# A four-layer mixer with float32 products: layer norm roots computed with tokens on partitions and spread by TensorE, scaled chunks in a ring, the final norm's sums gathered during layer 1's output projection

## The chip, the core and the metric

The program runs on one core of one Trainium2 chip. The metric is the device time of one execution in microseconds (us); lower is better.

## What is computed

256 latent tokens and 256 context tokens (512 in all) of width 2048 go through four layers. Two layers come from a first block, then its output is normed once more (`final_g`), and two layers of a second block follow, with a fresh context. Each layer begins with the same modulated norm of both halves:

```
h_lat = rms_norm(x,  norm_g[l]) * (1.0 + scale)   + shift
h_ctx = rms_norm(xc, norm_g[l]) * (1.0 + scale_c) + shift_c
...                                  # input projections, attention, gates
x  = x  + gate   * (mixed @ w_out[l])
xc = xc + gate_c * (mixed_c @ w_out[l])      # not in a block's last layer
...
return rms_norm(x, final_g)          # end of the first block
```

`rms_norm(x, w)` is `x * rsqrt(mean(x * x) + 1e-6) * w`, with the mean over the 2048 features of a token. So between two layers there are three steps: a sum of squares over all features, one inverse root for each token, and a product with every element.

## The kernel before

Activations are held with features on partitions: `x_residual` (xT) is 16 chunks of 128 features by 512 tokens, context tokens first. Each product with a weight is done in three passes for precision (a high and a low part of both operands), `three`, L1294. Weights come in slots of 128x1024 elements: the sync engine (SP) loads a slot into `w_raw` (a ring of 4), ScalarE (ACT) copies it to `w_high` (L547, `high(n)`), VectorE (DVE) subtracts to get `w_low` (L849, `low(n)`), and TensorE (PE) multiplies. `w_high` and `w_low` are rings of 2, so that `high(n)` waits until PE has used slot n-2. A group of four slots makes two output tiles. Every engine has its own stream, written out in the order of the list of phases that `plan_phases` makes; semaphores tie the streams together.

Between layers the phases are these:

- `linear` "out" (four rounds of two groups). After each group DVE adds the gated result to xT (L1170), squares two chunks (L1181) and adds them to a running sum in `tmp` (L1185). After the last group it folds two halves into one (L1221), and PE multiplies the sum by a matrix of ones (L1563): this sums over partitions and leaves the sum in every partition of PSUM `scores`, 128x512.
- `store` writes xT's latent half to `x_scratch` in device memory (ACT's queue, L824), to be read back in the next layer's `ysplit`.
- `root`: ACT makes mean and root of all 128x512 elements (`mean_and_root`, L559 and L560), DVE takes the reciprocal and one Newton step (`inverse_root`, L876 to L887).
- `apply`, for each of 16 chunks: DVE scales xT in place (`scale_chunk`, L922), ACT adds the shift and makes `h_high` (L605), DVE makes `h_low` (L932). Weight slots 1 to 5 of the next projection are split in between (`split_beside`).

The order of layer 1's end is longer. A root for the final norm, the final norm's product with all 16 chunks (L1108), the store, then a new pass of squares over the normed x (phase "ms": ACT L738, PE L1499, 16 chunks in turn), then the root of layer 2.

In `opening` the first layer does the same with squares from ACT (L623) and 16 products with ones (L1514), in between the first modulation products (L1345, L1355); the copy L555 stands on ACT behind the first shifted chunks and two weight slots.

The first q projection's round takes its slots in the order `PAIRED`; its slots 0 to 5 are split ahead, and the slot with index 6 is split by the first `high` and `low` behind `apply`:

```
for k in range(8):
    if 8 * i + k >= ph["ahead"]:
        high(n0 + 8 * i + k + 1)
```

## Time and profile before

| | us |
|---|---|
| runs shown, median (lowest to highest) | 3244.1 (3240.6 to 3244.69) |
| the profiled execution, its own time | 3241.01 |
| its span in the trace | 3239.1 |
| PE busy | 3027.7 (93% of the span) |
| DVE busy | 1605.7 (50%) |
| ACT busy | 1023.4 (32%) |
| POOL busy | 102.0 (3%) |

The span is the stretch from the first to the last instruction of the profiled execution. PE is busy nearly throughout. All rows below are from that one execution; their times are us from the span's start.

### The profile page before, as it was taken

How to read it: one execution, taken by the hardware profiler on the slowest of the kernel's cores; microseconds unless marked ns; L12 is line 12 of the kernel's file. 1: busy time of each engine (PE TensorE's matmuls, PEld its weight loads, DVE VectorE, ACT ScalarE, POOL GpSimd, SP SyncE). 2: the span in 40 equal slices, each digit the busy share in tenths (PEclk: the TensorE clock that was granted, in tenths of full speed). 3: DMA queues.
4: the chain of work that ended last, by engine and by line, in shares of the span. 5: the costliest groups of instructions: out<-in, count | busy, mean ns of one | idle time of the engine just before them, and what ended most of it. 6: DMA issues, size and time to landing. Idle time of an engine off the chain costs nothing. (4 is left out here: it accounts for less than half of the span.)

```text
span 3239.1 us, 40895 instructions
## 1 busy us (share of the span) xinstructions
PE 3027.7 (93%) x17158; PEld 2362.8 (73%) x17158; DVE 1605.7 (50%) x2493; ACT 1023.4 (32%) x1508; POOL 102.0 (3%) x157
## 2 busy tenths in 40 slices
PE   5899999999997999999878999999999979999988
PEld 1577777785675787886766779766776758798888
DVE  2334333355435554454556373555473455747574
ACT  2212233223312332332323221334342123315453
POOL 0000000000000000000000000240000000003100
PEclk7899999999998999999989999999999989999999
DMA  8644433221543643741763444333445433222455
GB/s 321 274 169 143 144 130 130 98 73 45 183 174 137 227 176 121 268 132 65 272 225 126 154 151 166 132 111 111 150 158 206 163 116 117 85 92 92 137 169 169
DMA packets 120135, 495.10 MB, mean 153 GB/s; under 512 B 11792, under 2 KB 30480, under 8 KB 95120
## 3 DMA queue, kind: packets, MB, share of 16 engines
q1 hardware_dynamic: 99648, 463.51, 40.2%
q10 hardware_dynamic: 20304, 28.97, 2.6%
q8 instruction: 136, 2.23, 0.3%
q14 instruction: 47, 0.39, 0.0%
HBM read 484.05 MB, written 8.39 MB: 152 GB/s over the span
## 5 line engine op out<-in xcount | busy, mean ns | idle before, releaser
L1294 PE MATMUL products<-h_high,w_high 128*128 128x512 f32 (+1 forms) x3424 | 1256.2, 367 | 91.4 <-DVE h_low L932 47.1
L1294 PE MATMUL products<-h_low,w_high 128*128 128x512 f32 (+1 forms) x3424 | 1189.7, 347 | 0.0
L1294 PE MATMUL products<-h_high,w_low 128*128 128x512 f32 (+1 forms) x3424 | 1189.2, 347 | 0.0
L849 DVE TENSOR_TENSOR w_low<-w_raw,w_high 128x1024 fp32r<-128x1024 f32 x500 | 615.3, 1231 | 819.6 <-ACT w_high L547 817.1
L547 ACT CAST w_high<-w_raw 128x1024 fp32r<-128x1024 f32 x500 | 522.9, 1046 | 1382.4 <-PE products L1294 1333.8
L1294 PEld LDWEIGHTS products<-h_high,w_high 128*128 128x128 f32 x3424 | 657.3, 192 | 341.9 <-issue 228.0
L1294 PEld LDWEIGHTS products<-h_low,w_high 128*128 128x128 f32 x3424 | 659.0, 192 | 81.0 <-issue 13.0
L1294 PEld LDWEIGHTS products<-h_high,w_low 128*128 128x128 f32 x3424 | 657.4, 192 | 81.6
L1294 PE MATMUL products<-w_high,h_high 128*128 128x256 f32 x640 | 184.1, 288 | 0.5 <-issue 0.5
L1294 PE MATMUL products<-w_high,h_low 128*128 128x256 f32 x640 | 181.1, 283 | 0.0
L1294 PE MATMUL products<-w_low,h_high 128*128 128x256 f32 x640 | 181.0, 283 | 0.0
L876 DVE RECIPROCAL tmp<-tmp 128x512 f32<-128x512 f32 (+2 forms) x35 | 133.3, 3809 | 76.4 <-ACT tmp L560 76.4
L1369 PE MATMUL modulation<-ada_w,cond_silu 128*32 128x512 f32 x1264 | 169.0, 607 | 0.0
L670 ACT ACTIVATE tmp<-scores,softmax_stats,q_root 128x512 f32<-128x512 f32 (+1 forms) x144 | 101.5, 708 | 174.5 <-DVE softmax_stats L1017 174.5
L1294 PEld LDWEIGHTS products<-w_high,h_high 128*128 128x128 f32 x640 | 122.7, 192 | 13.1 <-issue 12.3
L1294 PEld LDWEIGHTS products<-w_high,h_low 128*128 128x128 f32 x640 | 122.8, 192 | 1.0 <-issue 1.0
L1294 PEld LDWEIGHTS products<-w_low,h_high 128*128 128x128 f32 x640 | 122.7, 192 | 0.0
L1010 DVE TENSOR_REDUCE softmax_stats<-scores 128x1 f32<-128x512 f32 (+1 forms) x144 | 86.0, 597 | 60.9 <-PE scores L1436 37.5
L1023 DVE RECIPROCAL softmax_stats<-softmax_stats 128x1 f32<-128x1 f32 x192 | 26.5, 159 | 163.7 <-ACT tmp L670 163.7
L510 POOL COPY pool_values<-mix_a 128x512 f32<-128x512 f32 (+1 forms) x16 | 12.2, 765 | 2912.1 <-DVE mix_a L1159 2910.7
L657 ACT COPY tmp<-turned 128x512 f32<-128x512 f32 (+1 forms) x96 | 49.3, 514 | 169.2 <-PE turned L1448 169.2
L605 ACT ACTIVATE h_high<-x_residual,ada 128x256 fp32r<-128x256 f32 x128 | 56.7, 500 | 90.3 <-DVE x_residual L922 90.3
(193 smaller groups left out, 2676.9 us busy)
## 6 DMA issues: line engine op xcount, KB each, us to landing
w_raw<-w_slots SPq DMA_DIRECT2D x500, 512.0 KB, 3.5
ada_w<-ada_slots SPq DMA_DIRECT2D x174, 1024.0 KB, 6.0
mix_b<-ada_slots SPq DMA_DIRECT2D x18, 1024.0 KB, 9.8
x_residual<-x ACTq DMA_DIRECT2D x2, 4096.0 KB, 23.0
x_scratch<-x_residual ACTq DMA_DIRECT2D x3, 2048.0 KB, 8.0
x_residual<-x_scratch ACTq DMA_DIRECT2D x3, 2048.0 KB, 9.2
x_residual<-ctx ACTq DMA_DIRECT2D x2, 2048.0 KB, 16.2
out<-x_residual ACTq DMA_DIRECT2D x1, 2048.0 KB, 7.8
```

What stands on the lines that cost most here:

```text
L510: step(nc.gpsimd.tensor_copy(pool_v[:, seg, PAD:PAD + S], v))
L547: nc.scalar.copy(whi[:, n % SPL, :], raw[:, n % RAW, :]).then_inc(high_done, 1)
L605: last = nc.scalar.activation(hh[:, t, tk], xT[:, t, tk], ACT.Identity, bias=adaT[:, r, c + st:c + st + 1])
L657: nc.scalar.copy(dst[:, 0:nk], src[:, 0:nk]).then_inc(pt_done, 1)
L670: nc.scalar.activation(tmp[:, t0 + c % ring, 0:nk], src, ACT.Exp, scale=a["scale"] if a["wide"] else q_rs[:, k:k + 1], bias=stat[:, c % 8, ...
L849: nc.vector.tensor_tensor(wlo[:, n % SPL, :], raw[:, n % RAW, :], whi[:, n % SPL, :].bitcast(F32), ALU.subtract).then_inc(low_done, 1)
L876: step(nc.vector.reciprocal(r, r))
L1010: step(nc.vector.reduce_max(stat[:, c % 8, 0:1], src, AX.X))
L1023: step(nc.vector.reciprocal(stat[:, c % 8, 3:4], stat[:, c % 8, 2:3]))
L1294: ins = nc.tensor.matmul(o, a, b, start=first and q == 0, stop=last and q == 2, skip_group_check=skip)
L1369: ins = nc.tensor.matmul(AD[32 * j:32 * j + 32, :], sc32[:, k, :], place[:, j * 512:(j + 1) * 512], start=k == 0, stop=k == KC - 1)
```

## The change

1. **Sums.** A matmul has one operand held in the array (the weights) and one that moves through it. Before, the ones were held and the squares moved, 512 columns. Now each 128x128 tile of squares is held and one column of ones moves (`token_sums`): a token's sum lands on one partition, and the sums of 512 tokens are 128x4 numbers.
2. **Roots.** Mean, root and inverse are computed on 128x4 numbers. PE then spreads them to all partitions, with a column of `x_root` repeated as the held operand and the identity moving (`x_broadcast`), and ACT copies the 128x512 result from PSUM to `tmp`.
3. **Last group of an output projection.** Its two chunks are not added to the running sum. ACT squares one, DVE the other, and PE sums them directly; the fold L1221 is gone. ACT issues a small root ahead, on `eps`.
4. **Ring.** `scale_chunk` writes to a ring of four pieces of `tmp` (`xs`) and leaves xT as it was. The wait for the store moves from `apply` to the kv or k projection.
5. **Final norm.** During layer 1's output projection ACT also squares each latent chunk times its final gain, and DVE adds these to `gained` (in `pool_sums`). From the two sums DVE gets the combined inverse root of both norms for the latent half, and the final norm's own. The phases "ms" and one of the two roots are gone. The final norm's product with xT (16 instructions) and the store now stand behind layer 2's `apply`.

The core of the diff (semaphores, tiles and phase bookkeeping are left out):

```diff
+            def x_root(layer):
+
+                n = 6 if layer == 2 else 4
+
+                nc.scalar.activation(stat[:, 7, 3:4], eps_col[:, 0:1], ACT.Sqrt)
+                act.wait_ge(x_var, layer + 1)
+                nc.scalar.activation(x_rs[:, 0:n], x_ms[:, 0:n], ACT.Sqrt).then_inc(x_rooted, 1)
+
+                act.wait_ge(x_spread, layer + 1)
+                nc.scalar.copy(tmp[:, 2, :], SC[:, 1, :]).then_inc(x_ready, 1)
...
@@ -748,6 +737,10 @@
                     for t in range(KC):
                         shift_chunk(layer, t, at["apply"] + t + 1)
                         split_beside(pi, t, high)
+                    if layer == 2:
+
+                        act.wait_ge(x_final, KC)
+                        act.dma_start(dram["x_scratch"], xT[:, :, LAT]).then_inc(x_out, 16)
                 elif kind == "linear":
...
+                        if ph["evac"] == "res" and ph["layer"] == 1:
+
+                            g = 2 * i + j
+                            if g > 1:
+                                act.wait_ge(x_gain_sum, g - 1)
+                            for t in range(2):
+                                c = COL["final"] + 2 * g + t
+                                if g < 2 * ph["pairs"] - 1:
+                                    act.wait_ge(freed_dve, 2 + at["fd"] + g + 1)
+                                else:
+                                    act.wait_ge(x_tile, 2 * ph["layer"] + t + 1)
+                                    if t == 0:
+
+                                        nc.scalar.activation(tmp[:, 0, :], xT[:, 2 * g, :],
+                                                             ACT.Square).then_inc(x_tile_sq, 1)
+                                dst = gained[:, t, :] if g == 0 else tmp[:, 4, t * S:(t + 1) * S]
+                                nc.scalar.activation(dst, xT[:, 2 * g + t, LAT], ACT.Square,
+                                                     scale=cols[:, c:c + 1]).then_inc(x_gained, 1)
+                            return
+                        if ph["evac"] == "res" and ph["layer"] < LAYERS - 1 and 2 * i + j == 2 * ph["pairs"] - 1:
+
+                            act.wait_ge(x_tile, 2 * ph["layer"] + 1)
+                            nc.scalar.activation(tmp[:, 0, :], xT[:, 4 * i + 2, :], ACT.Square).then_inc(x_tile_sq, 1)
+                            return
...
             def scale_chunk(t):
                 for st in range(2):
-                    x = xT[:, t, st * S:(st + 1) * S]
-                    last = nc.vector.scalar_tensor_tensor(x, x, mod_scale[:, t, st:st + 1],
-                                                          tmp[:, 2, st * S:(st + 1) * S], ALU.mult, ALU.mult)
+                    tk = slice(st * S, (st + 1) * S)
+                    last = nc.vector.scalar_tensor_tensor(xs(t)[:, tk], xT[:, t, tk], mod_scale[:, t, st:st + 1],
+                                                          tmp[:, 2, tk], ALU.mult, ALU.mult)
                 last.then_inc(scaled, 1)
+
+            def x_root(layer):
+
+                v, r = x_ms[:, 0:4], x_rs[:, 0:4]
+                dve.wait_ge(x_sums, layer + 1)
+                if layer != 2:
+                    nc.vector.tensor_scalar(v, SC[:, 0, 0:4], 1.0 / D, EPS, ALU.mult, ALU.add).then_inc(x_var, 1)
+                else:
+
+                    step(nc.vector.tensor_scalar(x_ms[:, 0:2], SC[:, 0, 0:2], 1.0 / D, EPS, ALU.mult, ALU.add))
+                    step(nc.vector.tensor_scalar(x_ms[:, 4:6], SC[:, 0, 2:4], 1.0 / D, EPS, ALU.mult, ALU.add))
+                    step(nc.vector.tensor_scalar(x_ms[:, 2:4], SC[:, 0, 4:6], 1.0 / D, None, ALU.mult))
+                    own()
+                    nc.vector.scalar_tensor_tensor(x_ms[:, 2:4], x_ms[:, 4:6], EPS, x_ms[:, 2:4], ALU.mult,
+                                                   ALU.add).then_inc(x_var, 1)
+                    v, r = x_ms[:, 0:6], x_rs[:, 0:6]
+                dve.wait_ge(x_rooted, layer + 1)
+                inverse_root(r, v).then_inc(x_inverse, 1)
 
             def low_chunk(layer, t, done):
...
+
+                    dve.wait_ge(ada_ready, columns_ready(layer, 2))
+                    scales(layer, 0, KC)
+                    if layer == 2:
+                        own()
+                        g = COL["final"]
+                        step(nc.vector.tensor_tensor(mod_scale[:, :, 1], mod_scale[:, :, 1], cols[:, g:g + KC],
+                                                     ALU.mult))
+                    x_root(layer)
                 elif kind == "apply":
                     layer = ph["layer"]
                     own()
-                    if ph["name"] == "final":
+                    dve.wait_ge(x_ready, layer + 1)
+                    for t in range(KC):
+                        scale_chunk(t)
+                        dve.wait_ge(scaled, at["apply"] + t + 1)
+                        if t >= 1:
+                            low_chunk(layer, t - 1, PARTS[pi] + t)
+                        split_beside(pi, t, low)
+                    low_chunk(layer, KC - 1, PARTS[pi] + KC)
+                    if layer == 2:
                         for t in range(KC):
                             x, c = xT[:, t, LAT], COL["final"] + t
-                            nc.vector.scalar_tensor_tensor(x, x, cols[:, c:c + 1], tmp[:, 2, LAT], ALU.mult,
-                                                           ALU.mult).then_inc(scaled, 1)
-                    else:
-
-                        dve.wait_ge(ada_ready, columns_ready(layer, 2))
-                        scales(layer, 0, KC)
-                        own()
-
-                        dve.wait_ge(x_out, 16 * layer)
-                        for t in range(KC):
-                            scale_chunk(t)
-                            dve.wait_ge(scaled, at["apply"] + t + 1)
-                            if t >= 1:
-                                low_chunk(layer, t - 1, PARTS[pi] + t)
-                            split_beside(pi, t, low)
-                        low_chunk(layer, KC - 1, PARTS[pi] + KC)
+                            nc.vector.scalar_tensor_tensor(x, x, cols[:, c:c + 1], SC[:, 0, LAT], ALU.mult,
+                                                           ALU.mult).then_inc(x_final, 1)
                 elif kind == "linear":
                     n0, par0, toks = at["slot"], at["group"] % 2, ph["toks"]
...
 
                                 dve.wait_ge(freed_dve, 2 + at["fd"] + g + 1)
-                                first = g == 0
-                                if not first and not (g == 1 and at["xsq"] == 0):
-                                    dve.wait_ge(x_summed, at["xsq"] + g - 1)
-                                sq = tmp[:, 2:4, :] if first else tmp[:, 0:2, :]
-                                nc.vector.tensor_tensor(sq, xg[:, g, :, :], xg[:, g, :, :],
-                                                        ALU.mult).then_inc(x_squared, 1)
-                                if not first:
-                                    dve.wait_ge(x_squared, at["xsq"] + g + 1)
+                                if g > 0 and at["xsq"] + g - 1 > 0:
+                                    dve.wait_ge(x_summed, at["xsq"] + g)
+                                sq = tmp[:, 2:4, :] if g == 0 else tmp[:, 0:2, :]
+                                done = nc.vector.tensor_tensor(sq, xg[:, g, :, :], xg[:, g, :, :], ALU.mult)
+                                if g == 0:
+                                    done.then_inc(x_summed, 1)
+                                else:
+                                    done.then_inc(x_squared, 1)
+                                    dve.wait_ge(x_squared, 6 * layer + g)
                                     nc.vector.tensor_tensor(tmp[:, 2:4, :], tmp[:, 2:4, :], sq,
                                                             ALU.add).then_inc(x_summed, 1)
+                            if layer == 1 and g < 2 * ph["pairs"] - 1:
+
+                                dve.wait_ge(x_gained, 2 * g + 2)
+                                if g > 0:
+                                    if g > 1:
+                                        dve.wait_ge(x_gain_sum, g - 1)
+                                    nc.vector.tensor_tensor(gained, gained,
+                                                            tmp[:, 4, :].rearrange("p (t n) -> p t n", t=2),
+                                                            ALU.add).then_inc(x_gain_sum, 1)
                         else:
 
...
+            def token_sums(a, col, first):
+
+                for tt in range(a.shape[-1] // P):
+                    ins = nc.tensor.matmul(SC[:, 0, col + tt:col + tt + 1], a[:, tt * P:(tt + 1) * P], ONES[:, 0:1],
+                                           start=first and tt == 0, stop=True, skip_group_check=True)
+                return ins
+
+            def x_broadcast(layer):
+
+                pe.wait_ge(x_inverse, layer + 1)
+                for tt in range(4):
+                    ins = nc.tensor.matmul(SC[:, 1, tt * P:(tt + 1) * P], x_rs[:, tt:tt + 1].to_broadcast([P, P]),
+                                           IDENT, start=True, stop=True)
+                if layer == 2:
+                    for tt in range(2):
+                        ins = nc.tensor.matmul(SC[:, 0, S + tt * P:S + (tt + 1) * P],
+                                               x_rs[:, 4 + tt:5 + tt].to_broadcast([P, P]), IDENT,
+                                               start=True, stop=True)
+                ins.then_inc(x_spread, 1)
+
...
-
-                        pe.wait_ge(x_summed, at["xsq"] + 2 * ph["pairs"])
-                        nc.tensor.matmul(SC[:, 0, :], ONES, tmp[:, 2, :], start=True, stop=True).then_inc(ms_done, 1)
+                        layer, g = ph["layer"], 2 * ph["pairs"] - 1
+
+                        pe.wait_ge(x_summed, at["xsq"] + g)
+                        token_sums(tmp[:, 2, :], 0, True)
+                        token_sums(tmp[:, 3, :], 0, False)
+                        if layer == 1:
+
+                            pe.wait_ge(x_gain_sum, g - 1)
+                            for t in range(2):
+                                token_sums(gained[:, t, :], 4, False)
+                        pe.wait_ge(x_tile_sq, layer + 1)
+                        token_sums(tmp[:, 0, :], 0, False)
+                        if layer == 1:
+                            pe.wait_ge(x_gained, 2 * g + 2)
+                            for t in range(2):
+                                token_sums(tmp[:, 4, t * S:(t + 1) * S], 4, False)
+                        pe.wait_ge(freed_dve, 2 + at["fd"] + g + 1)
+                        token_sums(tmp[:, 1, :], 0, False).then_inc(x_sums, 1)
+                elif kind == "root":
+                    x_broadcast(ph["layer"])
```

**DVE, end of layer 1's output projection to layer 2's first chunk.** This is the order before, from the last group's gated addition on (`ada` and `gain_cols` are modulation and gains):

```order
L1170 SCALAR_TENSOR_TENSOR x_residual<-products,ada,x_residual 128x256 x2
L1181 TENSOR_TENSOR tmp<-x_residual 128x1024
L1185 TENSOR_TENSOR tmp<-tmp 128x1024
L1221 TENSOR_TENSOR tmp<-tmp 128x512
L876 RECIPROCAL tmp<-tmp 128x256
L878 TENSOR_TENSOR tmp<-tmp 128x256
L885 SCALAR_TENSOR_TENSOR tmp<-tmp 128x256
L887 SCALAR_TENSOR_TENSOR tmp<-tmp 128x256
L1108 SCALAR_TENSOR_TENSOR x_residual<-x_residual,gain_cols,tmp 128x256 x16
L876 RECIPROCAL tmp<-tmp 128x512
```

And this is the same place in the changed kernel:

```order
L1209 SCALAR_TENSOR_TENSOR x_residual<-products,ada,x_residual 128x256 x2
L1216 TENSOR_TENSOR tmp<-x_residual 128x512
L930 SCALAR_TENSOR_TENSOR mod_scale<-ada,gain_cols 128x16 x2
L1141 TENSOR_TENSOR mod_scale<-mod_scale,gain_cols 128x16
L948 TENSOR_SCALAR x_mean_square<-scores 128x2
L949 TENSOR_SCALAR x_mean_square<-scores 128x2
L950 TENSOR_SCALAR x_mean_square<-scores 128x2
L952 SCALAR_TENSOR_TENSOR x_mean_square<-x_mean_square 128x2
L890 RECIPROCAL x_root<-x_root 128x6
L892 TENSOR_TENSOR x_mean_square<-x_mean_square,x_root 128x6
L899 SCALAR_TENSOR_TENSOR x_mean_square<-x_mean_square,x_root 128x6
L901 SCALAR_TENSOR_TENSOR x_root<-x_mean_square,x_root 128x6
```

The wide instructions between the gated addition and the first chunk have become narrow ones, and the 16 of the final norm are no longer there.

**ACT, end of layer 2's `apply`.** Before (`h_high` is a shifted chunk, `w_high` a weight slot):

```order
L605 ACTIVATE h_high<-x_residual,ada 128x256 x6
L547 CAST w_high<-w_raw 128x1024
L605 ACTIVATE h_high<-x_residual,ada 128x256 x4
L547 CAST w_high<-w_raw 128x1024 x2
L570 ACTIVATE tmp<-products 128x1024
```

and in the changed kernel:

```order
L597 ACTIVATE h_high<-tmp,ada 128x256 x6
L539 CAST w_high<-w_raw 128x1024
L597 ACTIVATE h_high<-tmp,ada 128x256 x4
L743 DMA x_scratch<-x_residual 2048x1x256
L539 CAST w_high<-w_raw 128x1024 x2
L562 ACTIVATE tmp<-products 128x1024
```

The store has come between the last shifted chunk and the split of the slot with index 6; it waits for DVE's 16 final products.

**PE, from layer 1's last product to layer 2's first.** Before, the sum over partitions, then the 16 sums of phase "ms":

```order
L1294 MATMUL products<-h_high,w_low 128x256
L1563 MATMUL scores<-tmp,consts 128x512
L1499 MATMUL scores<-tmp,consts 128x256 x16
L1294 MATMUL products<-h_high,w_high 128x512
L1294 MATMUL products<-h_low,w_high 128x512
```

and in the changed kernel:

```order
L1344 MATMUL products<-h_high,w_low 128x256
L1389 MATMUL scores<-consts,tmp 128x1 x8
L1389 MATMUL scores<-consts,pool_sums 128x1 x4
L1389 MATMUL scores<-consts,tmp 128x1 x12
L1397 MATMUL scores<-consts,x_root 128x128 x4
L1401 MATMUL scores<-consts,x_root 128x128 x2
L1344 MATMUL products<-h_high,w_high 128x512
```

24 one-column sums and six spreading products stand where 17 wide ones stood.

## Rows read from the trace of the kernel before

**Rows 1.** Waits of PE: engine, line, waited for: us in total, times, longest.

```profile
PE products L1294 <- DVE h_low L932: 47.1, 11, 11.8
PE scores L1499 <- ACT tmp L738: 13.8, 1, 13.8
```

**Rows 2.** Timeline between layers 0 and 1: start, duration in us, engine, instruction, [idle before].

```profile
1023.56 0.61 ACTq L824 DMA_DIRECT2D x_scratch<-x_residual  x1
...
1026.08 0.69 DVE L1221 TENSOR_TENSOR tmp<-tmp 128x512 f32<-128x512 f32 x1
...
1026.83 2.08 PE L1563 MATMUL scores<-tmp,consts 128*128 128x512 f32 x2 [5.00 <-DVE tmp L1221]
...
1029.63 1.28 ACT L560 ACT_TABLE_LOAD   x1
...
1031.65 3.35 DVE L876 RECIPROCAL tmp<-tmp 128x512 f32<-128x512 f32 x1 [4.87 <-ACT tmp L560]
...
1037.69 1.80 DVE L922 SCALAR_TENSOR_TENSOR x_residual<-x_residual,mod_scale,tmp 128x256 f32<-128x256 f32 x4
...
1040.70 0.55 PE L1294 MATMUL products<-h_high,w_high 128*128 128x256 f32 x1 [11.79 <-DVE h_low L932]
```

**Rows 3.** Timeline of PE between layers 2 and 3.

```profile
2651.78 0.55 PE L1294 MATMUL products<-h_high,w_high 128*128 128x256 f32 x1 [11.80 <-DVE h_low L932]
```

**Rows 4.** Timeline between layers 1 and 2.

```profile
1674.72 2.08 PE L1563 MATMUL scores<-tmp,consts 128*128 128x512 f32 x2 [4.21 <-DVE tmp L1221]
...
1682.39 6.42 DVE L1108 SCALAR_TENSOR_TENSOR x_residual<-x_residual,gain_cols,tmp 128x256 f32<-128x256 f32 x16
...
1688.85 0.59 ACTq L824 DMA_DIRECT2D x_scratch<-x_residual  x1
...
1690.01 0.72 ACT L738 ACTIVATE tmp<-x_residual 128x256 f32<-128x256 f32 x2 [10.93 <-issue]
...
1712.90 0.77 PE L1294 MATMUL products<-h_high,w_high 128*128 128x512 f32 x1 [10.39 <-DVE h_low L932]
```

**Rows 5.** Timeline of the opening.

```profile
41.19 14.88 PE L1514 MATMUL scores<-tmp,consts 128*128 128x512 f32 x32
...
64.39 3.26 DVE L922 SCALAR_TENSOR_TENSOR x_residual<-x_residual,mod_scale,tmp 128x256 f32<-128x256 f32 x8
...
71.02 1.87 PE L1355 MATMUL modulation<-select,tmp 128*128 128x4 f32 x8 [11.38 <-ACT tmp L555]
```

**Rows 6.** Timeline at other places: operations like the new ones.

```profile
165.53 1.84 PE L1400 MATMUL scores<-consts,tmp 128*128 128x1 f32 x16
...
1545.30 1.06 PE L1456 MATMUL turned<-tmp,v_mla 128*128 128x128 f32 x8
...
1829.16 0.31 ACT L560 ACTIVATE q_root<-scores,eps 128x64 f32<-128x64 f32 x1
...
1829.54 0.55 DVE L876 RECIPROCAL q_root<-q_root 128x64 f32<-128x64 f32 x1
...
1830.90 0.20 DVE L982 TENSOR_SCALAR q_root<-q_root 128x64 f32<-128x64 f32 x1
```

**Rows 7.** Groups by form on ACT: shapes xcount | busy us, mean ns | idle.

```profile
L555 ACT COPY tmp<-modulation 128x512 f32<-128x512 f32 x18 | 10.5, 585 | 48.7 <-PE modulation L1345 48.6 <-issue 0.2
```

**Rows 8.** Timeline at the end of layer 2's apply.

```profile
1750.28 1.22 DVE L849 TENSOR_TENSOR w_low<-w_raw,w_high 128x1024 fp32r<-128x1024 f32 x1 [0.33 <-ACT w_high L547]
...
1752.79 1.05 ACT L547 CAST w_high<-w_raw 128x1024 fp32r<-128x1024 f32 x1 [2.55 <-PE products L1294]
```

**Rows 9.** Stretches: us, busy PE, PEld, DVE, ACT, POOL, granted clock, DMA share, GB/s.

```profile
1714.00:1716.00 2.00, 2.00 (x6) 1.56 (x5) 1.96 (x6) 1.20 (x4) 0.00 (x0) 0.50 0.03 8
1716.00:1718.00 2.00, 2.00 (x8) 1.61 (x7) 1.01 (x2) 1.13 (x2) 0.00 (x0) 0.78 0.00 0
```

**Rows 10.** Timeline of layer 1's output projection, around two groups' ends.

```profile
1604.19 1.22 DVE L849 TENSOR_TENSOR w_low<-w_raw,w_high 128x1024 fp32r<-128x1024 f32 x1
...
1605.60 1.04 ACT L547 CAST w_high<-w_raw 128x1024 fp32r<-128x1024 f32 x1 [1.82 <-PE products L1294]
...
1615.81 1.22 DVE L849 TENSOR_TENSOR w_low<-w_raw,w_high 128x1024 fp32r<-128x1024 f32 x1
...
1617.08 0.39 PE L1294 MATMUL products<-h_high,w_high 128*128 128x256 f32 x1 [0.75 <-DVE w_low L849]
```

92 lines of the change are left out of this document (36 added, 56 removed).

## The prediction

> **What bounds the kernel now.** I read the waits of PE first, since PE is busy nearly throughout (the table above). Its largest wait is for the first chunks of a layer, 47.1 us in 11 waits, and a single one of 13.8 us stands before the squares of layer 2 [rows 1]. The timelines show that they belong to three gaps, in which PE does nearly nothing. Between layers 0 and 1 the last product ends at 1026.83 - 5.00 = 1021.83 and the first of the next layer starts at 1040.70: 18.87 us [rows 2]. Between layers 2 and 3 the wait before the first product is the same (11.80 against 11.79), so I take the same gap [rows 3]. Between layers 1 and 2 it is 1712.90 - (1674.72 - 4.21) = 42.39 us [rows 4]. The opening has a fourth: from the end of the sums at 56.07 to the first scaled chunk at 64.39, 8.32 us, and PE's column product at 71.02 waits for ACT, which stands behind that chunk [rows 5]. The change works on these four places, so its worth is what it takes out of them, less what it puts elsewhere.
>
> **Between layers 0 and 1, and 2 and 3.** Time zero is PE's last product.
> - The gated additions end at 1.73, when the store is issued (1023.56) [rows 2]. The new square of the last chunk on DVE (0.69, from the like 128x512 instruction of rows 2) ends at 2.45. The store now waits for it.
> - ACT issues the store, 0.61, until 3.05. From the end of the other store's issue (1689.44) to ACT's next instruction (1690.01) there are 0.57 [rows 4]: 3.6. Then the table load that the first root brings, 1.28 [rows 2], until 4.9, the root on eps and the real root at 0.31 each [rows 6]: 5.5.
> - PE meanwhile does 16 one-column sums. Eight such cost 1.84 [rows 6], so 3.7; DVE's scaling of 128x4 adds 0.2 (the like instruction L982 of [rows 6]): 3.9, hidden under ACT's 5.2. A sum of four one-column products costs as much (0.92) as the 512 wide one did: 14.88 / 16 = 0.93 in the opening [rows 5]. Nothing is gained on PE itself.
> - The inverse: on 128x64 it took 1830.90 - 1829.54 = 1.36 with 0.55 for the reciprocal [rows 6]. For 128x4 I take 1.0: 6.5. Bounds: four instructions at 0.2 (0.8), and 1.36.
> - Spreading: four 128x128 products cost 1.06 at the full clock [rows 6]: 7.55. At half clock, as the 2.08 for one 512 wide product shows against 0.93, it would be 2.1.
> - ACT's copy from PSUM 0.59 [rows 7]: 8.15, four handovers between engines at 0.05: 8.35.
> - First scaled chunk to first product as before, 1040.70 - 1037.69 = 3.01 [rows 2]: 11.35.
>
> So 18.87 becomes 11.35, a gain of 7.5 each, 15.0 together; with the bounds 6.1 to 7.9 each. The table load is on this path. In the trace the next root and the reciprocal follow so close on it (1029.63 + 1.28 + 0.69 = 1031.60 against 1031.65) that nothing else is spent.
> The Trainium skill (ScalarE: Activation LUTs, What ACT_TABLE_LOAD costs) gives 1283 ns for the load, as here, but adds a drain of about 1380 ns to each switch. The trace does not show that drain; by the page each of these two gaps would be 1.4 us longer, 2.8 in all.
>
> **Between layers 1 and 2.** No store stands in this path now. PE does 24 one-column sums, 24 x 0.23 = 5.5, and the earlier ones are ready in time. DVE's four small instructions 0.8 (6.3), root 0.31 (6.6), inverse 1.0 (7.6), six spreading products 1.6 (9.2), copy 0.59 and handovers 0.2 (10.0), then 3.0: 13.0. The table load lies under the sums. 42.39 becomes 13.0, a gain of 29.4. Three things go against it:
> - *The moved final norm.* In `apply` nothing changes per chunk: the ring of four has each place free by the order of the streams. But behind the last chunk DVE does 16 products (6.42) [rows 4], ACT waits for them, issues the store (0.59), needs 0.57 to its next instruction, and only then casts the slot with index 6 (1.05). DVE would have been free at 1750.28 - 0.33 = 1749.95 [rows 8], so `low` starts at 1749.95 + 6.42 + 0.59 + 0.57 + 1.05 + 0.1 = 1758.7 and ends at 1759.9. PE finished index 5 at about 1752.75, as the next cast shows [rows 8]. A new wait of 7.15 us, which nothing hides. What follows is set by PE, so it carries to the end.
> - *The clock.* After the gap PE's clock is 0.50 until about 1716.9 (0.78 in the stretch 1716 to 1718) [rows 9], 4 us after 1712.90, in which the time per product is nearly double: about 1.9 us lost. The new wait of 7 us should bring this once more: 1.9.
> - *Gained squares.* In layer 1's output projection DVE gets one more 128x512 addition (0.69, of which some 0.65 show) behind six of the eight groups, ahead of `low`. At odd groups PE already waits for that `low`, 0.75 at 1617.08; at even ones `low` ends at 1605.41 and PE needs it at about 1605.55 [rows 10]. So 3 x 0.65 + 3 x 0.5 = 3.5. ACT's two squares per group (about 0.8) lie under DVE's squares.
>
> Net: 29.4 - 7.15 - 1.9 - 3.5 = 16.8.
>
> **Opening.** The 16 sums take as long as before. Then 0.2, 0.31, 1.0, 1.06, 0.59 and 0.5 for handovers and PE's drain, 3.7 in place of 8.32; the table load starts with ACT's last square and ends about with the sums, so that I take 4.6 saved. PE's next modulation products move behind the spreading, some 2.8 later, but in the trace they were done long before 71.02. If the loads that they free become late, 2 of this is lost.
>
> **Sum.** 15.0 + 16.8 + 4.6 = 36.4 us from the profiled execution's 3241.0: 3204.6. The median of the runs shown is 3.1 above that execution; I take half of it and forecast 3206.
>
> **Rivals.**
> - *The final products do not stall PE* (8 in 100). They would have to fit before PE needs index 6. Against it stands the order of ACT's stream, in which that cast is behind the store. It would return 7.15 + 1.9 = 9.1: 3197.
> - *Handing on is dearer* (15 in 100). The new path crosses between engines more often than the old, with small instructions, so fixed costs decide. If spreading runs at half clock (+1.0 in each of four places), the inverse takes 1.36 (+0.36 each) and a handover 0.2 in place of 0.05 (+0.15 for five, in four places, 3.0), and the loads in the opening come 2 late, the gain is 36.4 - 4.0 - 1.4 - 3.0 - 2.0 = 26: 3216 to 3217.
> - *The coupling in layer 1's output projection turns it slower* (2 in 100). ACT's squares wait for DVE's additions, and the next cast stands behind them. If each group held PE up and its clock fell with that, as it does in the gaps, products would take about twice as long for much of this phase. It decides from a stall of some 5 us in each of seven groups, together with the clock: 7 x 5 = 35 eats the gain, and half clock for 60 of these us costs about 28 more: 3241 - 40 + 35 + 28 = 3264. Against it: casts have idle time of 1.8 us before them and the squares need 0.8 [rows 10].
> - *No change that can be told* (1 in 100): that the gaps shrink but apply, where DVE sets the pace in the layers with 256 tokens, takes it back. It starts earlier by the same amount, so I see no mechanism.
>
> **How the numbers follow.** The likeliest case has 74 in 100 and a range of its own of 3200 to 3212, from the bounds of inverse, spreading and extra addition. To hold 8 in 10 together with parts of the first two rivals: 3197 to 3217. A difference of 0.2% (6.5 us) is about what can be told from none. Faster 0.97, same 0.01, slower 0.02.
>
> **What would show it.** Right: no 128x512 reciprocal in the gaps; about 11.4 us from last to first product at layers 1 and 3 and 13.0 at layer 2; one wait of PE near 7 us for `w_low` about 40 us into layer 2, with the clock at 0.50 behind it; PE waits of about 1.4 in place of 0.75 in layer 1's output projection. Wrong: a clock of 0.50 during the sums or the spreading; a table load that holds back more than its 1.28; loads that PE waits for in the opening.

## The result

The changed kernel takes 3217.9 us (median of four runs, 3214.3 to 3221.6), against 3243.3 us for the kernel before (3240.6 to 3244.7): a ratio of 0.992, 95% interval 0.9905 to 0.9935. It is faster, by 25 us where 37 were forecast, and the median lies 0.9 us above the range. (A fourth run of the kernel before, 3242.4 us, has come to the runs of the table.) One execution of all those below was slow, one of the four of the kernel with 128 columns everywhere, at 5973.1 us and for a reason that the record does not show; that kernel's numbers go by the other three.

The profiled execution of the changed kernel took 3214.3 us, with a span of 3212.5 against 3239.1. It is the fastest of the four, 3.6 us below their median. In the groups' numbers below the lines of the code have moved: L1294 is now L1344, L849 is L863, L932 is L964, L922 is L936, L1170 is L1209. The 16 opening sums are 64 products of one column (128 records, as each float32 product leaves two), at L1389; the spreading is L1397.

On the page of the execution PE is busy for 3046.5 us, 95% of the span against 93% before:

```profile
PE 3046.5 (95%) x17364; PEld 2394.9 (75%) x17364; DVE 1580.6 (49%) x2497; ACT 1022.4 (32%) x1513; POOL 102.0 (3%) x157
```

The waits of PE next (engine, line, waited for: us in total, times, longest), the answer to [rows 1]:

```profile
PE products L1344 <- DVE w_low L863: 29.1, 17, 6.1
PE products L1344 <- DVE h_low L964: 23.4, 12, 3.8
```

The wait for the first chunks has halved (47.1 us before), the one of 13.8 us is gone, and a single one of 6.1 us for `w_low` is new. So the gaps went as meant. The opening is where they did not. Rows of its timeline (start, duration in us, engine, instruction, idle before), against [rows 5]:

```profile
41.61 24.17 PE L1389 MATMUL scores<-consts,tmp 128*128 128x1 f32 x128
45.36 0.63 ACT L626 ACTIVATE tmp<-x_residual 128x512 f32<-128x512 f32 x1 [0.26 <-PE scores L1389]
47.05 0.63 ACT L626 ACTIVATE tmp<-x_residual 128x512 f32<-128x512 f32 x1 [1.06 <-PE scores L1389]
65.87 0.16 DVE L945 TENSOR_SCALAR x_mean_square<-scores 128x4 f32<-128x4 f32 x1 [23.44 <-PEq L1579]
67.12 2.07 PE L1397 MATMUL scores<-consts,x_root 128*128 128x128 f32 x8 [1.34 <-DVE x_root L901]
69.85 3.26 DVE L936 SCALAR_TENSOR_TENSOR tmp<-x_residual,mod_scale,tmp 128x256 f32<-128x256 f32 x8 [2.79 <-ACT tmp L610]
76.49 1.06 PE L1425 MATMUL modulation<-select,tmp 128*128 128x4 f32 x8 [2.06 <-ACT tmp L547]
```

The sums take 24.17 us, where 14.88 stood in [rows 5]. The squares, of which each waits for the sum two before it, show when it happens: one every 0.89 us up to 45.36, and one every 1.70 us from then on. The windows of the same execution (stretch in us, busy time of PE, of its weight loads PEld, of DVE, ACT and POOL, the clock granted to TensorE as a share of 2.4 GHz, DMA share, GB/s), as in [rows 9], show what goes with it:

```profile
43.00:45.00 2.00, 2.00 (x20) 2.00 (x20) 0.00 (x0) 1.48 (x3) 0.00 (x0) 1.00 1.01 410
45.00:47.00 2.00, 2.00 (x12) 2.00 (x12) 0.00 (x0) 0.73 (x2) 0.00 (x0) 0.55 0.99 410
1032.00:1034.00 2.00, 1.62 (x7) 1.63 (x8) 0.28 (x2) 0.00 (x0) 0.00 (x0) 0.50 1.04 348
1672.00:1674.00 2.00, 2.00 (x17) 2.00 (x17) 0.00 (x0) 1.34 (x2) 0.00 (x0) 0.84 0.39 145
1674.00:1676.00 2.00, 2.00 (x11) 2.00 (x11) 0.00 (x0) 0.00 (x0) 0.00 (x0) 0.50 0.03 10
1731.00:1733.00 2.00, 1.51 (x4) 1.22 (x5) 2.00 (x3) 1.04 (x2) 0.00 (x0) 0.50 1.04 379
```

PE is busy for all of these two stretches at 43 to 47 us, and yet its granted clock falls from 1.00 (2.4 GHz) to 0.50 (1.2 GHz) between them. The same happens in the 24 sums of the gap between layers 1 and 2 (1672 to 1676), and the spreading at 1032.38 runs at 0.50. Now rows of the gaps, against [rows 2] and [rows 4], and of the new wait:

```profile
1026.20 3.74 PE L1389 MATMUL scores<-consts,tmp 128*128 128x1 f32 x32
1026.40 1.66 DVE L1209 SCALAR_TENSOR_TENSOR x_residual<-products,ada,x_residual 128x256 f32<-128x256 f32 x4 [3.70 <-PE products L1344]
1029.93 1.28 ACT L605 ACT_TABLE_LOAD   x1 [1.99 <-issue]
1031.22 0.20 ACT L605 ACTIVATE softmax_stats<-eps 128x1 f32<-128x1 f32 x1
1031.33 0.19 ACT L607 ACTIVATE x_root<-x_mean_square 128x4 f32<-128x4 f32 x1
1032.38 2.08 PE L1397 MATMUL scores<-consts,x_root 128*128 128x128 f32 x8 [2.43 <-DVE x_root L901]
1035.18 1.79 DVE L936 SCALAR_TENSOR_TENSOR tmp<-x_residual,mod_scale,tmp 128x256 f32<-128x256 f32 x4 [2.86 <-ACT tmp L610]
1038.19 0.55 PE L1344 MATMUL products<-h_high,w_high 128*128 128x256 f32 x1 [3.74 <-DVE h_low L964]
...
1669.76 0.88 DVE L1209 SCALAR_TENSOR_TENSOR x_residual<-products,ada,x_residual 128x256 f32<-128x256 f32 x2 [1.07 <-PE products L1344]
1672.15 4.15 PE L1389 MATMUL scores<-consts,tmp 128*128 128x1 f32 x24
1684.63 0.76 PE L1344 MATMUL products<-h_high,w_high 128*128 128x512 f32 x1 [3.75 <-DVE h_low L964]
...
1721.59 6.35 DVE L1158 SCALAR_TENSOR_TENSOR x_residual<-x_residual,gain_cols,scores 128x256 f32<-128x256 f32 x16
1727.97 0.59 ACTq L743 DMA_DIRECT2D x_scratch<-x_residual  x1
1731.49 0.79 PE L1344 MATMUL products<-h_high,w_high 128*128 128x512 f32 x1 [6.07 <-DVE w_low L863]
```

The first gap, from DVE's first gated addition to the first product, has 1038.19 - 1026.40 = 11.79 us (1040.70 - 1021.87 = 18.83 before, from the same event). The second has 1684.63 - 1669.76 = 14.87 (1712.90 - 1670.54 = 42.36 before), and the third 11.76. No 128x512 reciprocal is left in them. At 1721.59 the 16 final products stand ahead of the cast and the split of the slot with index 6, and PE waits 6.07 us for it at 1731.49, with a clock of 0.50 behind (the window 1731 to 1733).

With starts of both kernels at these events, the 26.6 us between the spans fall as follows (after against before; what was predicted in brackets): the opening until the last product of layer 0, 4.5 lost (4.6 gained); first gap, 7.0 gained (7.5); layer 1 from first product to last, 1669.76 - 1038.19 = 631.57 against 1670.54 - 1040.70 = 629.84, 1.7 lost (3.5); second gap, 27.5 gained (29.4); layer 2 with the third gap, from product to product 940.12 against 938.88, 1.2 lost (7.5 - 7.15 - 1.9, so 1.55 lost); layer 3, 0.4 lost (nothing). Of the 9.8 us missing from 36.4, 9.1 stand in the opening with layer 0. The other terms are off by up to 1.9 us in both directions and nearly cancel.

One trace tells such a stretch only within some us: in four traces whose opening has the same code (the changed kernel and the runs below that leave the opening alone) DVE's last gated additions of layer 0 start at 1026.40, 1028.56, 1030.10 and 1031.61. The changed kernel's own is the earliest of them, so that its opening costs 4.5 us in this trace and up to 9.7 in the others.

### The profile page after: what moved, and what is told of

Read it like the earlier page. It is cut to its first block and busy times, and to the rows that moved or that the text cites. A ratio compares the mean times of both kernels' runs of the same rounds, so it can differ in the third digit from the quotient of the medians.

```text
span 3212.5 us, 41299 instructions
## 1 busy us (share of the span) xinstructions
PE 3046.5 (95%) x17364; PEld 2394.9 (75%) x17364; DVE 1580.6 (49%) x2497; ACT 1022.4 (32%) x1513; POOL 102.0 (3%) x157
## 5 line engine op out<-in xcount | busy, mean ns | idle before, releaser
L1344 PE MATMUL products<-h_high,w_high 128*128 128x512 f32 (+1 forms) x3424 | 1255.5, 367 | 78.4 <-DVE w_low L863 24.2
L1344 PE MATMUL products<-h_high,w_low 128*128 128x512 f32 (+1 forms) x3424 | 1188.8, 347 | 0.0
L1344 PE MATMUL products<-h_low,w_high 128*128 128x512 f32 (+1 forms) x3424 | 1188.6, 347 | 0.0
L863 DVE TENSOR_TENSOR w_low<-w_raw,w_high 128x1024 fp32r<-128x1024 f32 x500 | 615.0, 1231 | 816.4 <-ACT w_high L539 813.9
L1344 PEld LDWEIGHTS products<-h_high,w_high 128*128 128x128 f32 x3424 | 657.4, 192 | 326.8 <-issue 198.6
L1344 PEld LDWEIGHTS products<-h_low,w_high 128*128 128x128 f32 x3424 | 659.3, 193 | 80.9 <-issue 13.0
L1344 PEld LDWEIGHTS products<-h_high,w_low 128*128 128x128 f32 x3424 | 657.2, 192 | 81.4
L1344 PE MATMUL products<-w_high,h_high 128*128 128x256 f32 x640 | 184.1, 288 | 0.5 <-issue 0.5
L1344 PE MATMUL products<-w_high,h_low 128*128 128x256 f32 x640 | 181.1, 283 | 0.0
L1344 PE MATMUL products<-w_low,h_high 128*128 128x256 f32 x640 | 181.0, 283 | 0.0
L890 DVE RECIPROCAL tmp<-tmp 128x512 f32<-128x512 f32 (+2 forms) x30 | 118.2, 3939 | 30.4 <-ACT tmp L552 30.4
L1344 PEld LDWEIGHTS products<-w_high,h_high 128*128 128x128 f32 x640 | 122.7, 192 | 13.1 <-issue 12.3
L1344 PEld LDWEIGHTS products<-w_high,h_low 128*128 128x128 f32 x640 | 122.8, 192 | 1.0 <-issue 1.0
L1344 PEld LDWEIGHTS products<-w_low,h_high 128*128 128x128 f32 x640 | 122.7, 192 | 0.0
L597 ACT ACTIVATE h_high<-tmp,ada 128x256 fp32r<-128x256 f32 x128 | 56.7, 500 | 65.7 <-DVE tmp L936 65.7
```

Source lines behind the costliest of these rows:

```text
L597: last = nc.scalar.activation(hh[:, t, tk], xs(t)[:, tk], ACT.Identity, bias=adaT[:, r, c + st:c + st + 1])
L863: nc.vector.tensor_tensor(wlo[:, n % SPL, :], raw[:, n % RAW, :], whi[:, n % SPL, :].bitcast(F32), ALU.subtract).then_inc(low_done, 1)
L890: step(nc.vector.reciprocal(r, r))
L1344: ins = nc.tensor.matmul(o, a, b, start=first and q == 0, stop=last and q == 2, skip_group_check=skip)
```

## Experiments

Theory A: in the opening it is the one-column products that the clock falls with, and this makes the miss. Rivals: B, the loads or weights behind set the opening's end, and the miss lies elsewhere; C, it is the loading of new weights for every product; D, in the gaps it is the idle time of PE. All times are medians of kernels run on the same chip as the kernel before; each ratio is to that.

**The opening as before.** Only the opening goes back: 16 products by ones of 512 columns, and a root and inverse root on 128x512.

```diff
-                                last = token_sums(tmp[:, t % 2, :], 0, t == 0).then_inc(ms_done, 1)
-                            pe.wait_ge(ms_done, KC)
-                            nc.tensor.drain().then_inc(x_sums, 1)
-                            x_broadcast(0)
+                                nc.tensor.matmul(SC[:, 0, :], ONES, tmp[:, t % 2, :], start=t == 0,
+                                                 stop=t == KC - 1).then_inc(ms_done, 1)
```

> The changed kernel with layer 0's opening as it was before (16 products by ones of 512 columns, root and inverse root on 128x512); everything behind it stays changed. Theory A (the miss lies in the opening: the one-column sums run at half clock): the sums take 14.9 us again instead of 24.2, the first scaled chunk stands at about 64.4 us instead of 69.9, layer 0's last product comes about 4.5 us earlier, and the time falls by about 4.5 us, to about 3213 us. Rival B (the opening costs nothing, since the loads of the weights set the end of it, and the miss lies in the gaps and in layer 1's output): the time stays at 3218 us within 1.

Measured: 3212.0 us (3211.7 to 3214.2), ratio 0.9907 (0.9893 to 0.9922). The timeline of its opening, with a clock of 1.00 in the whole stretch 41 to 56:

```profile
41.77 14.88 PE L1579 MATMUL scores<-tmp,consts 128*128 128x512 f32 x32
64.96 3.26 DVE L938 SCALAR_TENSOR_TENSOR tmp<-x_residual,mod_scale,tmp 128x256 f32<-128x256 f32 x8
```

So the old opening, with its reciprocal on 128x512, is 5.9 us better than the new one, and no execution of either kernel lies among the other's. B falls: what the opening loses is missing from the whole time.

**128 columns of ones in the opening.** The same 64 sums, with the same 64 loads of weights, but each with 128 columns in place of one.

```diff
-                                last = token_sums(tmp[:, t % 2, :], 0, t == 0).then_inc(ms_done, 1)
+                                for tt in range(4):
+                                    k = slice(tt * P, (tt + 1) * P)
+                                    last = nc.tensor.matmul(SC[:, 0, k], tmp[:, t % 2, k], ONES,
+                                                            start=t == 0 and tt == 0, stop=True,
+                                                            skip_group_check=True)
+                                last.then_inc(ms_done, 1)
```

> The changed kernel, in whose opening each of the 64 sums has 128 columns of ones instead of one (the same weights are loaded as often; the result is read from every 128th column). Theory A (products of one column let the clock fall though TensorE is busy throughout): the granted clock stays at 1.00, 64 sums take about 15 us, the first scaled chunk stands at about 61 us and the time falls by 7 to 9 us, to about 3210 us. Rival C (it is the loading of new weights for every product, or something else in this stretch, that the clock falls with): the sums take 24 us or more and the time stays at 3218 us or rises.

Measured: 3206.9 us (3204.5 to 3209.6), ratio 0.989 (0.9876 to 0.9905). Its opening, and a window of it:

```profile
42.09 15.19 PE L1579 MATMUL scores<-consts,tmp 128*128 128x128 f32 x128
58.62 1.16 PE L1397 MATMUL scores<-consts,x_root 128*128 128x128 f32 x8 [1.34 <-DVE x_root L901]
60.43 3.25 DVE L936 SCALAR_TENSOR_TENSOR tmp<-x_residual,mod_scale,tmp 128x256 f32<-128x256 f32 x8 [1.87 <-ACT tmp L610]
```

```profile
45.00:47.00 2.00, 2.00 (x19) 1.98 (x19) 0.00 (x0) 1.26 (x2) 0.00 (x0) 1.00 1.02 418
```

128 times the columns, and the sums take 15.19 us instead of 24.17. The clock stays at 1.00 and the spreading, behind the same 1.34 us of idle time, takes 1.16 instead of 2.07. A holds for the opening and C falls. This is also the kernel that the prediction priced: with the sums at their old length it takes 3206.9 us, where 3206 was forecast. That the two meet within 1 us is in part luck, as the other terms' errors cancel.

**DVE adds the squares, PE goes on with modulation.** ACT's squares go into a ring of four, DVE adds them into one chunk, and 4 sums replace 64. The products of the next modulation block come before them on PE.

```diff
+                            nc.vector.tensor_tensor(tmp[:, 2, :], tmp[:, 2, :], tmp[:, XS[(t - 1) % 4], :],
+                                                    ALU.add).then_inc(open_added, 1)
...
-                        for u in range(8 * c, 8 * c + 8):
+                        for u in range(12 if c == 1 else 8 * c, 8 * c + 8 + 4 * (c == 0)):
...
+                            pe.wait_ge(open_added, KC - 1)
+                            token_sums(tmp[:, 2, :], 0, True).then_inc(x_sums, 1)
```

> The changed kernel, in whose opening VectorE adds up the squares while TensorE goes on with the next four modulation units, and only one chunk is summed over features, by 4 one-column products instead of 64. Theory A: 15 additions of about 0.65 us bring the end of the sums from 65.8 to about 53 us, the first scaled chunk to about 57 us (from 69.9), the loads go on in the 15 us in which they stood still, and the time falls by 9 to 13 us, to 3205 to 3209 us. Rival B (the loads, or the wait for the weights, set the end of the opening): the first scaled chunk comes early all the same, but the time falls by less than 4 us.

Measured: 3202.6 us (3200.3 to 3203.9), ratio 0.9875 (0.9858 to 0.9891), 15.3 us below the changed kernel and more than forecast. Its opening, and two windows (the last three numbers are granted clock, DMA share and GB/s):

```profile
42.28 11.83 DVE L984 TENSOR_TENSOR tmp<-tmp 128x512 f32<-128x512 f32 x15
61.48 3.25 DVE L939 SCALAR_TENSOR_TENSOR tmp<-x_residual,mod_scale,tmp 128x256 f32<-128x256 f32 x8 [2.79 <-ACT tmp L610]
```

```profile
45.00:47.00 2.00, 1.72 (x8) 0.20 (x8) 1.74 (x3) 1.50 (x4) 0.00 (x0) 0.50 1.03 430
56.00:72.00 16.00, 11.57 (x62) 7.46 (x63) 11.44 (x36) 6.78 (x14) 0.00 (x0) 0.71 0.86 348
```

The first scaled chunk stands at 61.48, not at 57, and even later than with 128 columns (60.43). About 2 us of that are the additions, one every 0.79 us (11.83 / 15) instead of 0.65. Most of the rest is the clock: it is 0.50 already from 45 to 47 us, ten us before the first one-column sum (55.61) and behind a wait of 1.87 us for modulation weights. So the four sums take 1.84 us and the spreading 2.07, twice their time at full clock. In this opening it is not the one-column products that the clock falls with.

The kernel is 4.3 us faster than the one with 128 columns all the same, by medians whose executions lie apart. Two things differ, and the run does not part them. The loads go on, with a DMA share of 0.86 from 56 to 72 us, where the changed kernel moved 0 GB/s from 56 to 66. And PE does the next modulation units while DVE adds, so that layer 0's first product with a weight slot starts at 69.24 us instead of 76.79. PE's waits for modulation weights from 60 us on hardly differ (6.3 us here, 6.8 with 128 columns), which speaks for the second. So the opening's worth is not only the first scaled chunk, and this part of the gain I had not priced; that it comes from the loads is not shown.

**128 columns everywhere.** Every sum over features, behind layers 0, 1 and 2 too.

```diff
-                    ins = nc.tensor.matmul(SC[:, 0, col + tt:col + tt + 1], a[:, tt * P:(tt + 1) * P], ONES[:, 0:1],
+                    ins = nc.tensor.matmul(SC[:, col // 4, tt * P:(tt + 1) * P], a[:, tt * P:(tt + 1) * P], ONES,
                                            start=first and tt == 0, stop=True, skip_group_check=True)
```

> The changed kernel with 128 columns of ones in every sum over features, in the opening and behind layers 0, 1 and 2. Theory A (only products of so few columns let the clock fall): the opening as in the run with 128 columns (15.2 us); the 24 sums behind layer 1 take 5.5 us instead of 6.7, since the clock stays at 1.00 to their end, and the gap shrinks from 14.9 to about 13.7; the spreading still stands behind some 2 us in which TensorE does nothing, and takes 2.1 at half clock where that is what it falls with, or 1.1. Time 3203 to 3206 us, so 1 to 4 below the opening alone. Rival D (in the gaps the idle time, not the one column, sets the clock): the gaps stay as they are, and the time at 3207 us.

Measured: 3202.0 us (3200.6 to 3204.3), ratio 0.987 (0.9853 to 0.9886). The first gap and its windows:

```profile
1015.95 3.84 PE L1389 MATMUL scores<-consts,tmp 128*128 128x128 f32 x32
1016.15 1.66 DVE L1209 SCALAR_TENSOR_TENSOR x_residual<-products,ada,x_residual 128x256 f32<-128x256 f32 x4 [3.69 <-PE products L1344]
1022.12 1.16 PE L1397 MATMUL scores<-consts,x_root 128*128 128x128 f32 x8 [2.33 <-DVE x_root L901]
1024.01 1.80 DVE L936 SCALAR_TENSOR_TENSOR tmp<-x_residual,mod_scale,tmp 128x256 f32<-128x256 f32 x4 [1.95 <-ACT tmp L610]
```

```profile
1019.00:1021.00 2.00, 0.79 (x8) 0.60 (x6) 0.20 (x2) 1.32 (x2) 0.00 (x0) 1.00 0.62 211
1021.00:1023.00 2.00, 0.88 (x7) 0.88 (x8) 0.66 (x4) 0.26 (x2) 0.00 (x0) 1.00 1.04 346
```

PE is idle for 2.33 us before the spreading, as in the changed kernel (2.43), and the spreading takes 1.16 us at a clock of 1.00 instead of 2.08 at 0.50. The two kernels differ in nothing but the columns of the sums, so it is the one-column sums ahead of the idle time that cost the spreading its clock, and D falls for the spreading. It does not fall for the whole gap: here too the clock is 0.50 from 1025 to 1027, before the layer's first product and while PE waits 3.75 us for it. Gated addition to first product: 10.87 instead of 11.79, 12.31 instead of 14.87, and 10.83 instead of 11.76. That is 4.4 us in the trace; the medians of this kernel and of the one with 128 columns in the opening alone differ by 4.9. The time lies 1 us below the range expected. I had expected half of the second gap's gain and doubted that of the spreading.

**The final products in two halves.** 8 of them behind the split of slot 6 of layer 2's first round, 8 behind that of slot 7, and the store behind both. TensorE's first sums of squares of the heads, which share the PSUM bank of the final root, come behind them; without that wait nothing would order TensorE's writes to the bank and VectorE's reads of it.

```diff
+                            if ph["name"] == "q" and layer == 2 and i == 0 and k in (5, 6):
+                                for t in range(8 * (k - 5), 8 * (k - 5) + 8):
+                                    x, c = xT[:, t, LAT], COL["final"] + t
+                                    nc.vector.scalar_tensor_tensor(x, x, cols[:, c:c + 1], SC[:, 0, LAT],
+                                                                   ALU.mult, ALU.mult).then_inc(x_final, 1)
```

> The changed kernel with the final norm's 16 products on VectorE placed in two halves behind the splits of slots 6 and 7 of layer 2, the store of the result behind both on ScalarE's queue, and TensorE's first use of that PSUM bank by layer 2's heads behind them. Theory: the wait of 6.07 us at 1731.5 us goes down to 1 us or less and TensorE's clock does not fall a second time, so the time falls by 6 to 8 us, to about 3211 us. Rival: the same time is waited a slot or two later, before the squares of the first group; then the time falls by less than 2 us.

Measured: 3211.6 us (3208.8 to 3215.2), ratio 0.9899 (0.9884 to 0.9913), 6.3 below the changed kernel. DVE's row of work at this place now reads:

```profile
1724.47 1.23 DVE L862 TENSOR_TENSOR w_low<-w_raw,w_high 128x1024 fp32r<-128x1024 f32 x1 [0.33 <-ACT w_high L539]
1725.61 3.21 DVE L1260 SCALAR_TENSOR_TENSOR x_residual<-x_residual,gain_cols,scores 128x256 f32<-128x256 f32 x8
```

No product waits between 1715 and 1760, and layer 2's first product to layer 3's takes 2619.96 - 1687.11 = 932.85 us instead of 940.12. The stall and the clock behind it cost 7.3 us, 6.07 of them the stall itself, where the prediction had 7.15 + 1.9. The rival, that the wait would come back a slot or two later, falls.

**The table load ahead of the store.** ACT's root on eps, which brings the table, is placed before the wait for the store.

```diff
+                    if layer < LAYERS - 1:
+                        nc.scalar.activation(stat[:, 7, 3:4], eps_col[:, 0:1], ACT.Sqrt)
                     act.wait_ge(freed_dve, 2 + at["fd"])
```

> The changed kernel with ScalarE's root on eps (and so the load of the table of roots) ahead of the store behind layers 0 and 2, instead of behind it. Theory: the table load of 1.28 us lies under the last chunk's work; ScalarE's root then follows the scaling of the sums at once, and the two gaps of 11.8 us shrink by 1.0 to 1.3 us each: the time falls by 2 to 2.6 us, which the timing hardly tells, so the gaps in the trace decide. Rival (the table load is hidden already, and the sums set the time): both gaps stay at 11.8 us.

Measured: 3218.2 us (3214.5 to 3223.0), ratio 0.992 (0.9903 to 0.9936): no difference from the changed kernel. Its first gap:

```profile
1029.90 5.08 PE L1392 MATMUL scores<-consts,tmp 128*128 128x1 f32 x32
1031.74 1.28 ACT L839 ACT_TABLE_LOAD   x1
1035.01 0.16 DVE L948 TENSOR_SCALAR x_mean_square<-scores 128x4 f32<-128x4 f32 x1 [2.02 <-PE scores L1392]
1035.20 0.20 ACT L608 ACTIVATE x_root<-x_mean_square 128x4 f32<-128x4 f32 x1 [1.97 <-DVE x_mean_square L948]
```

The load is off the path, as the root follows the scaling at once. But here the clock fell already within the sums, which took 5.08 us instead of 3.74, and that ate the gain: the two gaps have 11.99 and 11.88 us (11.79 and 11.76 in the changed kernel), as the rival had it, though for another reason. In the seven traces with one-column sums behind layers 0 and 2 they took between 3.73 and 5.08; with 128 columns, 3.84 or 3.85. Whether moving the load has a part in the earlier fall is not shown, as other kernels have it too (5.08 with 128 columns in the opening alone). So the theory's size could not be read here, and was left to the last kernel.

**No gained squares.** ACT's scaled squares, DVE's additions and their sums in layer 1's output projection are left out.

> The changed kernel without the gained squares of layer 1's output projection: ScalarE's scaled squares, VectorE's additions and TensorE's 8 sums of them are left out, and the final norm takes other columns in their place. Theory (VectorE's addition ahead of each split holds TensorE up): the waits of 1.35 us at odd groups go back to 0.75 and the phase shortens by 1.5 to 3.5 us, the sums behind it by 2 us; time about 3213 to 3214 us. Rival (they are hidden, and the lead is lost elsewhere): the phase keeps its length, and the time falls by the 2 us of the sums alone.

Measured: 3216.7 us (3214.8 to 3218.4), ratio 0.9914 (0.9899 to 0.9928). The timing does not tell it from the changed kernel. In the traces layer 1 from first product to last gated addition is 629.55 us instead of 631.57, and the gap behind it 11.74 instead of 14.87. PE's waits at odd groups, first the changed kernel's, then this one's:

```profile
1615.69 0.39 PE L1344 MATMUL products<-h_high,w_high 128*128 128x256 f32 x1 [1.35 <-DVE w_low L863]
```

```profile
1619.50 0.38 PE L1316 MATMUL products<-h_high,w_high 128*128 128x256 f32 x1 [0.75 <-DVE w_low L844]
```

The wait is 0.75 us again, as in [rows 10], and two groups, from one such wait's end to the next, take 28.59 us instead of 29.18. So the extra addition shows by 0.6 us at odd groups and not at all at even ones. Together the two stretches are 5.1 us shorter. The profiled executions do not show it, since this one's opening was late: its first scaled chunk stands at 72.82 instead of 69.85 and layer 0 ends 5.2 us later, with the same code. By the medians the forecast of 3213 to 3214 us was missed.

**Four edits together.** DVE's additions in the opening, 128 columns everywhere, the final products in halves, and the table load ahead of the store.

> The changed kernel with four of the edits together: VectorE's additions and the next modulation units in the opening, 128 columns in every sum over features, the final products in two halves behind the splits of slots 6 and 7, and ScalarE's root on eps ahead of the stores. If they add up: 3202.6 (the opening alone) less 3.8 (128 columns in the gaps, the difference of the two runs with them) less 7.3 (the final products, from layer 2's first product to layer 3's) less 2 (the table load, which now no longer lies beside sums at half clock, 1.1 in each of two gaps) = 3189.5 us, within 3187 to 3193. Rival (the opening's gain was partly waiting in the loads, or the table load stays hidden as in the run with it alone): 3192 to 3197. In the trace, the first gap's gated additions to the first scaled chunk should take 6.8 us, against 7.9 with 128 columns alone.

Measured: 3188.3 us (3186.8 to 3190.6), ratio 0.9832 (0.9818 to 0.9846). It beats both kernels, by 54 and 30 us. In its first gap:

```profile
1010.69 1.66 DVE L1217 SCALAR_TENSOR_TENSOR x_residual<-products,ada,x_residual 128x256 f32<-128x256 f32 x4 [3.70 <-PE products L1357]
1014.37 0.16 DVE L950 TENSOR_SCALAR x_mean_square<-scores 128x4 f32<-128x4 f32 x1 [0.79 <-PE scores L1402]
1014.56 0.20 ACT L608 ACTIVATE x_root<-x_mean_square 128x4 f32<-128x4 f32 x1 [0.74 <-DVE x_mean_square L950]
1017.51 1.80 DVE L941 SCALAR_TENSOR_TENSOR tmp<-x_residual,mod_scale,tmp 128x256 f32<-128x256 f32 x4 [1.95 <-ACT tmp L611]
```

From gated addition to scaled chunk 6.82 us, against 7.86 with 128 columns alone: the table load is worth 1.04 once the sums no longer cover it. The time is within the forecast, 1.2 us below its sum, and the rival (3192 to 3197) falls. Its parts fit less well than the sum: against the trace of the kernel where DVE adds, the opening with layer 0 is 4.5 us shorter, for which nothing was counted, layer 1 is 3.3 longer, and layer 2 with the third gap 11.0 shorter, where about 9 were counted.

## Why the prediction was wrong

- *Opening: wrong, and nearly the whole miss.* The step that failed is "The 16 sums take as long as before". It was read from equal prices at full clock (0.92 us for four one-column products, 0.93 for a wide one). The price was right, since up to 45 us a sum takes 0.89. What I did not ask is whether the clock would stay, because in [rows 6] one-column sums come only eight at a time, behind wide products. Sixteen in a row are another thing: 24.17 us instead of 14.88. With 128 columns in them the same code gives 3206.9 us. The prediction's own sign of being wrong, a clock of 0.50 during the sums or the spreading, is what the traces show. The median adds 2.1 us to the miss: it lies 3.6 above the profiled execution, for 1.55 counted.
- *The root and its spreading: nearly right.* From the end of the sums (65.78) to the scaled chunk 4.07 us, for 3.7 predicted, in place of 8.32. Four small DVE instructions take 0.8 us and a handover some 0.05. The spreading takes 2.08 for 1.06 in three places and 2.93 for 1.6 in the second gap. I had this in a rival and left it out of the sum; it is three times 1.0 and once 1.3.
- *First and third gap: 7.0 each for 7.5.* The step that was wrong is the spreading (1.0 dearer); roots and inverse together were about 0.5 cheaper (0.3 and 0.8 us measured, for 0.6 and 1.0), which hides half of it. The table load was on the path, as predicted. The Trainium skill (ScalarE: Activation LUTs, What ACT_TABLE_LOAD costs) adds a drain of about 1380 ns to each switch; the root on eps starts at 1031.22, right behind 1029.93 + 1.28, so this trace does not show it either.
- *Second gap: 27.5 for 29.4.* The sums take 6.7 us where 5.5 were predicted and the spreading 2.9 where 1.6 were, both because of the clock. With 128 columns the gap is 12.31, for 13.0 predicted.
- *The new wait: right in place and cause, 6.07 for 7.15,* since PE was later at it than I had set: it stops 1731.49 - 6.07 - 1684.63 = 40.79 us behind the layer's first product, for 39.85. The chain on DVE and ACT was right: from the first final product to the end of `low` about 9.85 us, for 9.95. With the clock it cost 7.3 for 9.05, the clock's part being 1.2 for 1.9.
- *Gained squares: half of what was predicted, 1.7 for 3.5.* (2.0 by the run without them.) The even groups had room for the addition.
- *Rivals.* "Handing on is dearer" gave 3216 to 3217 and so nearly the measured time, but for other reasons: of its four parts only the spreading came true. (The loads did not hold PE up more: its waits for modulation weights in layer 0, from 60 us on, are 6.6 us against 7.6 before.) That the final products would not stall, that layer 1 would turn slower, and that nothing would change, did not happen.

The Trainium skill (TensorE: Matmul & The Clock Gate, Loop structure matters more than you think) gives products that stay back to back as the case in which the clock stays up. The sums are back to back here, PE's row is busy for 2.00 of 2.00 us, and the clock falls to 0.55 in that stretch; so for one-column products the measurement decides against it.

What stays open: whether the kernel where DVE adds gains by the loads or by the modulation products that PE does meanwhile, as both came at once; and what sets the 5 us by which layer 0 ends earlier or later from trace to trace with the same code.

## What to carry to other kernels

A row that is busy in the profile is no sign that TensorE keeps its clock: price a new stretch of many tiny products at both levels, and look at the granted clock of a stretch made of the same kind, as long as the new one, before you trust a price taken from a short one. If the weights' loading sets the pace anyway, more columns can be free, and here they were faster. And before taking a stretch out of an opening, look at what else could run beside it: here the weights' loads stood still from about 50 us to its end, and PE had modulation products to do.

## What was not expected of the hardware

- 64 float32 products of one column take 24.17 us (24.0 to 26.7 in four traces), and 64 of 128 columns with the same weights 15.19: 0.23 us each at a clock of 1.00, 0.43 at 0.50.
- The clock fell with one-column sums in a row although TensorE was busy throughout, and in 2.33 us of idle time behind sums of 128 columns it had not fallen yet.
